# Weights' high parts first in each unit, rounded gate sums, and an earlier rounding of their tables in a two-block model kernel

## The reference

```python
def short_conv_mixer(x_n, w_in, conv_w, w_out):
    b, c, h = jnp.split(x_n @ w_in, 3, axis=-1)
    return (b * causal_dwconv(c * h, conv_w)) @ w_out

def conv_ffn(x_n, w_up, conv_w, w_down):           # 1024 -> 2 x 2816 -> 1024
    g, u = jnp.split(causal_dwconv(x_n @ w_up, conv_w), 2, axis=-1)
    return (jax.nn.silu(g) * u) @ w_down

# first block, layer 0: mixer, FFN, and the keys and values shared with layer 1
ckv = rms_norm(h, kv_in_norm) @ w_dkv              # 256 + 64 (rotary)
kv = rms_norm(c_kv, kv_norm) @ w_ukv               # 8 heads, 128 + 128
# layer 1: latent attention, FFN
q = rms_norm(x_n @ w_dq, q_norm) @ w_uq            # 512 -> 8 heads x (128 + 64)
h = h + softmax(causal(q k^T * scale)) v @ w_o
h = h + conv_ffn(rms_norm(h, ffn_norm), ...)

# second block: gated linear attention in both directions, context first
q, k, v, r = split(a @ w_in)                       # 512, 512, 1024, 1024; 4 heads
z = (a @ w_a1[d]) @ w_a2[d] + b_a[d]               # d = 0, 1: the directions
log_a = log_sigmoid(z) / 16                        # gates, 4 heads x 128
b = cumsum(log_a)                                  # inside chunks of 64 tokens
q_dec = q * exp(b);  k_inv = k * exp(-b)
o = tril(q_dec k_inv^T) v + q_dec S
S = exp(b_last) * S + (k * exp(b_last - b))^T v
h = h + mod[2] * ((head_rmsnorm(o) * silu(r)) @ w_o)
h = h + mod[5] * (square(relu(modulate(rmsnorm(h), mod[3], mod[4]) @ mlp_w1)) @ mlp_w2)
return rmsnorm(h, final_g)
```

## Time and profile before

| | us |
|---|---|
| median of 3 runs | 931.51 (931.45 to 932.14) |
| the profiled execution | 932.7 |
| its span | 930.9 |
| TensorE busy | 919.4 (99%) |
| VectorE busy | 801.8 (86%) |
| ScalarE busy | 565.2 (61%) |

### The profile page before, as it was taken

How to read it: one execution, slowest core, us unless ns; L and a number is a source line. 1 busy time by engine, 2 the same in 40 slices (tenths; PEclk the granted TensorE clock), 3 DMA queues, 4 the chain that set the end, 5 groups by cost and what they waited for, 6 DMA issues and landing times.

```text
span 930.9 us, 19261 instructions
## 1 busy us (share of the span) xinstructions
PE 919.4 (99%) x6786; PEld 871.6 (94%) x6786; DVE 801.8 (86%) x1341; ACT 565.2 (61%) x934; POOL 1.8 (0%) x8
## 2 busy tenths in 40 slices
PE   8999999999999999999999999999999999999997
PEld 8999999999999899999999999988899988888886
DVE  7999899999989888899999987867868989886546
ACT  6645666666455566666666555879533668774343
POOL 0000000000000000000000000000000000000000
PEclk9999999999999999999999999999999999999999
DMA  8786675557676555555557676464675358778971
GB/s 309 251 275 219 189 278 200 190 182 273 249 276 211 166 184 177 175 188 184 191 188 263 236 268 204 159 226 158 222 239 197 98 177 270 237 236 205 268 217 58
DMA packets 64343, 197.68 MB, mean 212 GB/s; under 512 B 15934, under 2 KB 16446, under 8 KB 64160
## 3 DMA queue, kind: packets, MB, share of 16 engines
q1 hardware_dynamic: 64000, 195.88, 64.2%
q10 hardware_dynamic: 288, 1.05, 0.3%
HBM read 194.81 MB, written 1.05 MB: 210 GB/s over the span
## 4 chain that ended last, share of the span: by engine, by line
PE 87%; DVE 9%; ACT 2%; issue 1%; DMA 0%; ACTq 0%; DVEq 0%
PE ps L564 21%; PE ps L560 18%; PE ps L561 18%; PE ps L563 5%; PE ps L1053 3%; PE ps L1052 3%; PE ps L1054 3%; DVE wlo L1659 3%; PE ps L592 2%; PE ps L593 2%; PE ps L594 2%; ACT whi L1101 1%; PE ps L878 1%; DVE raw L1746 1%; DVE a L2169 1%
## 5 line engine op out<-in xcount | busy, mean ns | idle before, releaser
L1659 DVE TENSOR_TENSOR wlo<-raw,whi 128x1024 fp32r<-128x1024 f32 x301 | 365.2, 1221 | 77.7 <-ACT whi L1101 76.7
L1101 ACT ACTIVATE whi<-raw 128x1024 fp32r<-128x1024 f32 x301 | 315.4, 1052 | 109.7 <-DMA raw<-stream 36.5
L564 PE MATMUL ps<-x,wlo 128*128 128x256 f32 x1288 | 360.8, 280 | 0.0
L560 PE MATMUL ps<-x,whi 128*128 128x256 f32 x1064 | 299.5, 281 | 0.2 <-DVE wlo L1659 0.2
L561 PE MATMUL ps<-x,whi 128*128 128x256 f32 x1064 | 296.6, 279 | 0.0
L564 PEld LDWEIGHTS ps<-x,wlo 128*128 128x128 f32 x1288 | 242.2, 188 | 0.0
L560 PEld LDWEIGHTS ps<-x,whi 128*128 128x128 f32 x1064 | 200.0, 188 | 1.0 <-issue 0.5
L561 PEld LDWEIGHTS ps<-x,whi 128*128 128x128 f32 x1064 | 200.0, 188 | 0.6 <-issue 0.5
L564 PE MATMUL ps<-yhi,wlo 128*128 128x256 f32 x400 | 112.0, 280 | 0.0
L560 PE MATMUL ps<-yhi,whi 128*128 128x256 f32 x400 | 111.8, 280 | 0.0
L561 PE MATMUL ps<-ylo,whi 128*128 128x256 f32 x400 | 111.5, 279 | 0.0
(11 more groups left out here) (348 smaller groups left out, 1480.3 us busy)
## 6 DMA issues: line engine op xcount, KB each, us to landing
raw<-stream SPq DMA_DIRECT2D x341, 512.0 KB, 4.0
side<-stream SPq DMA_DIRECT2D x16, 512.0 KB, 4.7
raw<-stream SPq DMA_DIRECT2D x4, 256.0 KB, 5.5
c<-ctxT ACTq DMA_DIRECT2D x1, 1024.0 KB, 6.7
h_rows<-turned_h SPq DMA_DIRECT2D x32, 32.0 KB, 3.9
ct<-cst SPq DMA_DIRECT2D x1, 898.5 KB
rt_tab<-rot SPq DMA_DIRECT2D x1, 768.0 KB
out<-gained SPq DMA_DIRECT2D x2, 320.0 KB, 2.2
```

The lines of the kernel that those rows point to most:

```text
L560: pe.matmul(dst, whi[:, w], at(hi, k), start=(k == 0), stop=False)
L564: last = pe.matmul(dst, wlo[:, w], at(hi, k), start=False, stop=(k == K - 1))
L1101: c.sig(act.activation(whi[:, s * D:(s + 1) * D], raw[:, r * D:(r + 1) * D], ACT.Copy), hi_ready)
L1659: c.sig(dve.tensor_tensor(wlo[:, w], raw[:, r], whi[:, w], ALU.subtract), slots_done)
```

## The change

- **Two sweeps in a unit.** `units()` and `moving()` wait for whi alone (`rounded_unit`, on `hi_ready`), do the sixteen matmuls of whi for all eight blocks, then wait for wlo and do the eight of wlo. The units that are taken in pairs, the query units, the attention's out_chunk, three of gla_out, four of the MLP's units and mlp_down have code of their own and stay as they were.
- **Sums of the context's gates from rounded gates.** `ctx_exponents` goes with `gates_hi` and `gates_lo` and with `sums_r`, which gets 128 columns of ones: six rounded matmuls for each direction in place of three in float32. So the context's gates are rounded and split too. Direction 0's sums stand one unit later on TensorE.
- **Tables rounded earlier.** `sums_r` is made ahead of the tokens' first modulated chunk.
- **Attention's end.** ScalarE copies a unit's weights ahead of the table load; VectorE clears the sum and does the last head ahead of a remainder.

```diff
@@ -301,7 +301,7 @@
         sb("sums_held", 18 * GH * T + 56, F32, stage)
         gates_hi, gates_lo = [[sb(f"gates_{part}{d}", GH * T, F32R, stage) for d in range(2)] for part in ("hi", "lo")]
         sb("sums_pad", 8, F32, stage)
-        sums_r = sb("sums_r", 6 * P + 4, F32R, stage)
+        sums_r = sb("sums_r", 7 * P + 4, F32R, stage)
         stage.close()
         stage = ExitStack()
         sb("m_pad", 56, F32, stage)
@@ -517,6 +517,11 @@
                 c.n["unit"] = u + 1
                 return u % RING
+            def rounded_unit():
+                u, per = c.n.get("unit", 0), c.per.get("unit", 0)
+                pe.wait_ge(hi_ready, c.i * per + (u + 1) if per else u + 1)
+                return u % RING
+
             def halves_of(both, k):
                 return both[:, :].rearrange("p (s n) -> p s n", s=2)[:, :, k * T:(k + 1) * T]
@@ -545,7 +550,8 @@
                                 c.sig(last, pe_units)
                     blk, begin = 2 * K, 2
                 for j in range(begin, n):
-                    slot = slot_of_next_unit()
+                    slot = rounded_unit()
+                    blocks = []
                     for b in range(sizes[j % len(sizes)]):
                         t, k = tile[0] + blk // K, blk % K
                         if k == 0:
@@ -561,8 +567,11 @@
                             pe.matmul(dst, whi[:, w], at(lo, k), start=False, stop=False)
                         else:
                             pe.matmul(ps[t % lag][:, :], whi[:, w], halves_of(both, k), start=(k == 0), stop=False)
+                        blocks.append((dst, w, k))
+                        blk += 1
+                    slot_of_next_unit()
+                    for dst, w, k in blocks:
                         last = pe.matmul(dst, wlo[:, w], at(hi, k), start=False, stop=(k == K - 1))
-                        blk += 1
                     c.sig(last, pe_units)
                     if then is not None and j == after:
                         then()
@@ -591,7 +601,10 @@
                                 tile_free(t, RING)
                             pe.matmul(dst, hi[:, tok], whi[:, w], start=first, stop=False)
                             pe.matmul(dst, lo[:, tok], whi[:, w], start=False, stop=False)
-                            last = pe.matmul(dst, hi[:, tok], wlo[:, w], start=False, stop=final)
+                            blocks.append((dst, tok, w, final))
+                    slot_of_next_unit()
+                    for dst, tok, w, final in blocks:
+                        last = pe.matmul(dst, hi[:, tok], wlo[:, w], start=False, stop=final)
                     c.sig(last, pe_units)
                     if j in between:
                         between[j]()
@@ -832,22 +845,25 @@
             def ctx_exponents(d):
-                pe.wait_ge(ev("softplus"), d + 1)
+                pe.wait_ge(ev("gates_split"), d + 1)
+                pe.wait_ge(ev("sums_rounded"), 2)
                 pe.wait_ge(ev("gate_bank_read"), 2 + d)
-                inside = cst_of("sums_f")[:, 0:P] if d == 0 else cst_of("sums_b")[:, 2 * P:3 * P]
+                inside = sums_r[:, 0:P] if d == 0 else sums_r[:, 5 * P:6 * P]
+                ones_r = sums_r[:, 6 * P + 4:7 * P + 4]
                 for b in range(2):
                     alone = b != d
-                    last = pe.matmul(ps[5 + b][:, :], inside, zm[d][:, b * 512:(b + 1) * 512], start=True, stop=alone)
+                    here, other = slice(b * 512, (b + 1) * 512), slice((1 - b) * 512, (2 - b) * 512)
+                    pe.matmul(ps[5 + b][:, :], inside, gates_hi[d][:, here], start=True, stop=False)
+                    last = pe.matmul(ps[5 + b][:, :], inside, gates_lo[d][:, here], start=False, stop=alone)
                     if not alone:
-                        last = pe.matmul(ps[5 + b][:, :], ones, zm[d][:, (1 - b) * 512:(2 - b) * 512], start=False, stop=True)
+                        pe.matmul(ps[5 + b][:, :], ones_r, gates_hi[d][:, other], start=False, stop=False)
+                        last = pe.matmul(ps[5 + b][:, :], ones_r, gates_lo[d][:, other], start=False, stop=True)
                 last.then_inc(ev("ctx_expo"), 1)
             def exponents(d, m):
                 n = GH * d + m
-                pe.wait_ge(ev("gates_split"), d + 1)
-                if n == 0:
-                    pe.wait_ge(ev("sums_rounded"), 1)
+                pe.wait_ge(ev("gates_split"), 3 + d)
                 if n >= 3:
                     pe.wait_ge(ev("expo_read"), n - 2)
                 else:
@@ -893,9 +909,9 @@
             units(2, DC, xhi, xlo, chunks=x_ready)
             units(2, DC, xhi, xlo)
             pe.wait_ge(ev("gate_in"), 2)
-            units(2, DC, xhi, xlo)
+            units(3, DC, xhi, xlo)
             ctx_exponents(0)
-            units(2, DC, xhi, xlo)
+            units(1, DC, xhi, xlo)
             ctx_exponents(1)
             units(1, DC, xhi, xlo)
             gate_logits(1, 0)
@@ -1377,8 +1393,8 @@
                     head_hi(hd - 1)
             hi()
             head_hi(HEADS - 1)
+            hi()
             act.activation(spare[:, 0:1], ones[:, 0:1], ACT.Sqrt)
-            hi()
             sqrt_stat(D)
             c.n["tile_read"] += 8 + 4
             hi(2)
@@ -1433,8 +1449,8 @@
                 act.wait_ge(ev("gate_exp"), 2 * n + d + 1)
                 act.activation(za[d][:, :], za[d][:, :], ACT.Ln, bias=1.0).then_inc(ev("gate_ln"), 1)
-            def gates_rounded(d):
-                act.wait_ge(ev("softplus"), 3 + d)
+            def gates_rounded(n, d):
+                act.wait_ge(ev("softplus"), 2 * n + d + 1)
                 act.activation(gates_hi[d][:, :], zm[d][:, :], ACT.Copy).then_inc(ev("gates_rounded"), 1)
             def ctx_decays(d):
@@ -1481,6 +1497,10 @@
             act.activation(at(sq, 0), ps[7][:, 0:T], ACT.Sqrt, scale=1.0 / D, bias=EPS).then_inc(ev("first_root"), 1)
             gate_parts(0, 0)
             gate_bank_free(0)
+            act.wait_ge(ev("zc_lo"), DC)
+            sums_at = CST["sums_f"][0]
+            act.activation(sums_r[:, 0:6 * P + 4], ct[:, sums_at:sums_at + 6 * P + 4], ACT.Copy).then_inc(ev("sums_rounded"), 1)
+            act.activation(sums_r[:, 6 * P + 4:7 * P + 4], ones, ACT.Copy).then_inc(ev("sums_rounded"), 1)
             modulated(xhi, 0, (1, 2, 7))
             for tk in range(2):
                 c.sig(act.activation(ck[:, tk * 512:(tk + 1) * 512], result(4 if tk == 0 else 0, 512), ACT.Copy), tile_read)
@@ -1495,19 +1515,23 @@
             hi()
             gate_ln(0, 0)
             gate_ln(0, 1)
-            for m in range(1, GH):
-                queries(m)
-                hi()
+            queries(1)
+            hi()
+            gates_rounded(0, 0)
+            queries(2)
+            hi()
+            gates_rounded(0, 1)
+            queries(3)
+            hi()
             keys(0)
+            hi()
+            keys(1)
             ctx_decays(0)
             hi()
-            for m in range(1, 3):
-                keys(m)
-                hi()
+            keys(2)
+            hi()
             ctx_decays(1)
             keys(3)
-            sums_at = CST["sums_f"][0]
-            act.activation(sums_r[:, :], ct[:, sums_at:sums_at + 6 * P + 4], ACT.Copy).then_inc(ev("sums_rounded"), 1)
             hi()
             gate_parts(1, 0)
             hi()
@@ -1519,9 +1543,9 @@
             gate_ln(1, 0)
             gate_ln(1, 1)
             values_out(gv, 4, 0)
-            gates_rounded(0)
-            hi()
-            gates_rounded(1)
+            gates_rounded(1, 0)
+            hi()
+            gates_rounded(1, 1)
             hi()
             for m in range(0, GH, 2):
                 decays(0, m)
@@ -2144,10 +2168,10 @@
             dve.tensor_tensor(wa2r[64:GATE_ROWS, :], wa2s[64:GATE_ROWS, :], wa2r[64:GATE_ROWS, :], ALU.subtract)\
                 .then_inc(ev("gate_weights"), 1)
             head_lo(HEADS - 2)
+            clear_sum()
+            head_lo(HEADS - 1)
             lo()
-            head_lo(HEADS - 1)
             c.n["pe_units"] = PHASE_AT["attn_out"]
-            clear_sum()
             lo()
             reciprocal_root(rstd_c)
             lo()
@@ -2186,9 +2210,9 @@
                 dve.wait_ge(ev("gate_ln"), i + 1)
                 dve.tensor_tensor(zm[d][:, :], zm[d][:, :], za[d][:, :], ALU.add).then_inc(ev("softplus"), 1)
-            def gates_split(d):
-
-                dve.wait_ge(ev("gates_rounded"), d + 1)
+            def gates_split(n, d):
+
+                dve.wait_ge(ev("gates_rounded"), 2 * n + d + 1)
                 dve.tensor_tensor(gates_lo[d][:, :], zm[d][:, :], gates_hi[d][:, :], ALU.subtract).then_inc(ev("gates_split"), 1)
             def ctx_keys(d):
@@ -2261,6 +2285,7 @@
             softplus(0, 1)
             for n in range(2):
                 lo_and_dots(1)
+                gates_split(0, n)
                 final_norm(6 + n)
             lo_and_dots(3)
             ctx_keys(0)
```

(4 more changed lines are left out.)

## The result

| | before | changed |
|---|---|---|
| median, us (16 runs each) | 932.1 (931.31 to 934.03) | 934.01 (932.95 to 937.21) |
| ratio | | 1.0024 [1.0016, 1.0032] |
| profiled span, us | 930.9 | 932.0 |

The changed kernel is slower, by 1.9 us between the medians. The forecast was no change, 931.5, with a range of 930.4 to 932.8 and eight in ten for 929.2 to 933.6; the time lies above both. Of the 2.5 us between forecast and result, 0.6 is the base: the forecast added its sum to 931.51, a median of three runs, and sixteen runs of the same kernel give 932.1.

What follows compares the result with a forecast made beforehand. The prediction took TensorE, busy 919.4 of 930.9 us, as the bound: what it streams and where it stands. Terms +0.69 +1.1 -0.54 -0.78 -0.44 = +0.03 on 931.51 gave 931.5 us, range 930.4 to 932.8.

Steps and rivals of the forecast that it cites:

- (a): Start of up0: TensorE stops for chunk 7, wanted earlier in two sweeps; +0.69 us with the restart.
- (b): Start of dkv to the first query unit: stops for late chunks in two sweeps; +1.1 us, bounds +0.3 to +1.8.
- (c): Attention's end: earlier restart and no wlo stop, partly given back waiting for chunk 7 in up1; -0.54 us.
- (d): mlp_up: two stops, 0.37 and 0.41 us, go because whi was ready earlier; -0.78 us.
- (e): Gates' sums: rounded matmuls gain 2.34 us, ScalarE's later chain takes most back; -0.44 us, bounds -2.8 to +1.8.
- rival of absorbed stops: Chunked units' stops vanish in TensorE's pauses: 930.0 us, chance 0.10; with ScalarE in time in the gates 927.6, 0.14.
- broken stream: Rival: the wait inside each of 250 units costs a 0.10 us restart, 25 us in all, 956; chance 0.03.
- The first part: In (e): TensorE stands 1.65 us plus 0.1 restart for direction 0's late weights, after the unit ahead ends.
- rival of a wait for DMA: Gates: a weight tile ScalarE needs before the second decays is 2.27 us late, logits 1.8 later; 933.8 us, chance 0.11.

Runs made afterwards that it cites:

- e4: Changed kernel with the units that take activations chunk by chunk (first of up0, dkv, dq, up1) in one sweep as before; median 931.96 us, ratio 1.0005.
- e12: Changed kernel, chunked units in one sweep, tables rounded in ScalarE's idle time, direction 0's decays earlier, wlo four blocks behind whi in 28 mlp_up units; ratio 0.997.
- e9: Changed kernel with ScalarE's decays of direction 0 one key tile and one weight copy earlier; gates' stage 28.51 us instead of 29.87.
- e7: Changed kernel profiled a second time, no edit; 935.52 us in all, 2.84 us more in the gates.
- e10: Changed kernel with the tables rounded between the first root and first gate logits, where ScalarE stood idle; gates' stage 31.40 us.
- e5: Kernel before with mlp_down's scattered gate store replaced by eight 512-byte rows of another tile, gate's values left out; median 931.15 us, ratio 0.9989.
- e6: Changed kernel with mlp_down's scattered gate store replaced by eight 512-byte rows of another tile, gate's values left out; median 932.87 us, ratio to before 1.0011.
- e1: Kernel before with the two sweeps alone; gates' sums, tables and attention's end as before; ratio 1.003.
- e2: Kernel before with the gates' part alone: rounded sums, tables ahead of the tokens' chunks, direction 0 one unit later; ratio 1.0011.

## Why the prediction failed

The terms, changed kernel against before's second profile:

| | forecast | measured |
|---|---|---|
| (a) up0 | +0.69 | +0.68 |
| (b) dkv to the first query unit | +1.1 | +1.14 |
| (c) attention's end, up1 | -0.54 | -0.66 |
| (d) mlp_up, its 28 units | -0.78 | +0.03, second profile +0.04 |
| (e) gates | -0.44 | +0.41, second profile +3.25 |
| sum | +0.03 | +1.6, second +4.4 |

The sum is off by 1.6 us, and (d) and (e) are all of it, with 0.81 and 0.85 us: each left out a loss and put it at nothing.

- **(a), (b), (c) held**, with the restarts where they were forecast (100.65 for 100.7; the sum of (a) and (b) at the queries 1.8 for 1.8). e4 shows that the chunked units make (a) and (b): without two sweeps in them these go. The rival of absorbed stops falls, and so does that of a broken stream: a restart in each unit would show everywhere, and the 1632 matmuls of up1 and down1 take 196.84 us with the wait inside the unit and without.
- **(d), a step that failed by a term left out.** The stops did go, 0.97 us before and 0.07 now (each start distance less the mean step). I costed the new order in between at zero, "in steady state there is nothing to win", and not as a possible loss. Timelines of mlp_up, before, where a block's 512 and 256 columns alternate, and then the changed kernel:

```profile
800.19 0.39 PE L563 MATMUL ps<-x,whi 128*128 128x512 f32 x1
...
801.23 0.39 PE L563 MATMUL ps<-x,whi 128*128 128x512 f32 x1
```
```profile
800.89 1.32 PE L569 MATMUL ps<-x,whi 128*128 128x512 f32 x5
801.82 1.10 PE L569 MATMUL ps<-x,whi 128*128 128x512 f32 x4
802.75 0.64 PE L574 MATMUL ps<-x,wlo 128*128 128x256 f32 x4
```

  Before, three blocks take 1.04 us, 0.347 each. Now four matmuls of 512 take 0.93, 0.2325 each, and with one of 256 a block has 0.350. By the means over the 224 blocks: 224 x (0.2333 - 0.2284) = +1.10 us, the 256 columns 224 x (0.1175 - 0.1183) = -0.18, the stops -0.90, in all +0.02 for +0.03 measured (78.62 to 78.65 us). In the six other profiles of kernels with two sweeps in all of these units, the 512 columns step the same and the 256 columns at 0.1166 or 0.1167, and the units take 78.47 or 78.48: at best 0.15 us are won. The premise failed in a number that the trace had: I put 512 columns at twice 0.117, 0.234, where they took 0.228. By e12 the order has a part in it: with half of the blocks alternating a third of the loss came back, at the matmuls that alternate. What sets the step stays open; in the changed kernel a 512 behind the last 256 of the unit ahead takes 0.2340 too.
- **(e), the other step that failed.** "Direction 1's split ends at 611.7, wanted at 612.5: none." The split was in time: it ended at 610.85, and TensorE was through with the unit ahead at 611.7. But these sums also wait for `gate_bank_read`, which stands in the rows of the order: ScalarE's decays of direction 0, which now stand behind the two roundings of the gates, one more copy of weights and one more key tile. They began 25.78 us behind the stage's first matmul, 21.58 before, and the stop of 1.38 us is the wait for them. I had followed this wait for the logits and not for the sums. The first part was right in its sum and not in its form: 0.80 and 1.03 us of stops, together 1.83, for one of 1.75; the 0.80, for the small copy `spare`, was in no forecast. The terms close within 0.1 us: -2.38 for the sums' matmuls, -0.42 for the stop for wlo, +1.83, and +1.46 for the third stop with its restart are +0.49, for +0.41 measured.

  The cause is shown by e9: there the decays go ahead of that one copy and key tile and nothing else changes, they begin 1.38 us earlier, and the stop goes. (By its own figures the forecast should have had -0.50 and not -0.44, 617.1 against 617.60.)
- **The rival of a wait for DMA** was right in kind. In e7 and e10 a late tile stood in front of the same decays (1.34 and 0.94 us), and the stop grew to 2.6 and 2.3 us with a half clock behind it, which I had not priced. The stage lost 3.25 us in e7, where the rival had +1.8. A chance of 0.11 looks small: two of the nine profiles with the new gates show such a tile.
- **The measured 1.9 us** (1.7 without the store) is near the 1.6 of the profiles. The sixteen runs also hold slower ones. Two of them, 936.98 and 937.21 us, had a mean granted clock of 0.996, where the fourteen others had 0.998 to 1.000 and e7 with its half clock 0.997; 22 runs of the kernel before had 0.998 or more. So these two look like e7; in which stage they stood is not shown. Whether the stop at the store, in the mean 1.3 us longer in eight profiles of kernels with two sweeps and the scattered store (47.12 to 50.74) than in four without the sweeps (47.05 to 47.93), belongs to the change stays open; the times of e5 and e6 give it little, 1.0 against 1.1 us.

## What to carry to other kernels

- A wait moved inside a unit is paid where data comes in pieces: the last of eight pieces is wanted after 14 steps instead of 21, and the seven matmuls of wlo that lay in front of it lie behind it. Use the old order there (e4: 2.05 us back).
- When an operation on an engine's queue is moved, list every wait that its readers have, bank reuse too, and not only the new operand's.
- Don't difference two single profiles: take the time between the same instructions, stage by stage, and a second profile of each kernel.

## What was not expected of the hardware

- The context's sums, matmuls of 512 columns, stepped at 0.43 us in float32 and at 0.23 us rounded. A stop can cost what the rounding won: behind 2.47 us of idle time (e7) the rounded ones stepped at 0.43 us as well. The granted clock was 0.51 there, the level of 1.2 GHz; it was 0.50 behind 2.10 us (e10) and 0.50 behind 1.88 us (e1). It stayed at 1.00, 2.4 GHz, behind 1.70 us (e12), 1.58 us (e2) and 1.21 us (the changed kernel). (The Trainium skill, TensorE: Matmul & The Clock Gate, section "What's actually happening", names 1.2 GHz as the idle clock; the rows of e7 agree.)
- A store of 1024 single values of 4 bytes held up the tiles of weights around it: the tile issued 0.6 us ahead of it landed 7.0 to 11.4 us behind the store's issue (4.1 in e5, 3.6 in e6), and the store cost about 1 us in either kernel.
- The same code ran 1% slower for 190 us in one profile of fourteen, at a granted clock of 1.00; no run shows why.
